# First GEMM of a two-layer trunk: order of its loads, source of x's split, and where its norm's squares are summed

## The reference

```
def rms_norm(x, g):
    y = x * lax.rsqrt(jnp.mean(x * x, axis=-1, keepdims=True) + EPS)
    return y * g

u = rms_norm(h, norm_mix_g[0])              # h = x, 512 x 1024
proj = u @ w_in                             # 1024 x (512 + 256 + 32)
c_q, c_kv, k_r = proj[..., :512], proj[..., 512:768], proj[..., 768:]
q  = rms_norm(c_q, g_q) @ w_uq
kv = rms_norm(c_kv, g_kv) @ w_ukv
k_r = apply_rope(k_r, cos, sin)             # cos, sin from positions
```

## Time and profile before

| | |
|---|---|
| median of the runs | 1299.8 us |
| profiled execution | 1299.99 us, its span 1298.2 us |
| busy share of the span | PE 95%, VectorE 52%, ScalarE 35%, GpSimd 22% |
| chain that ended last | PE 79%, VectorE 8%, issue 6%, ScalarE 3%, GpSimd 2% |
| granted TensorE clock, mean | 0.975 |
| PE busy in the first of 40 slices (32.5 us each), and in the second | 0.6, 0.8 |

### The profile page before, as it was taken

One profiled execution on the slowest core, in us unless ns is written; L12 is line 12 of the kernel. 1 busy time (PEld: TensorE's weight loads), 2 busy tenths in 40 slices (PEclk: granted clock), 3 DMA queues, 4 the chain that ended last, 5 costly groups with the idle time before them and its releaser, 6 DMA issues.

```text
span 1298.2 us, 15828 instructions
## 1 busy us (share of the span) xinstructions
PE 1231.2 (95%) x5829; PEld 1016.0 (78%) x5829; DVE 675.5 (52%) x958; ACT 455.1 (35%) x725; POOL 281.1 (22%) x252
## 2 busy tenths in 40 slices
PE   6889999899999999999999998889999999999997
PEld 5667777678888888888889986676888888888885
DVE  6867888744533434434457544974443343343432
ACT  4336666543212212222343235652322221221232
POOL 4222222222201102002112134552220020110211
PEclk8999999899999999999999998988999999999998
DMA  5201011222233332232233331011323223223221
GB/s 159 60 22 28 23 26 25 94 68 94 97 98 97 98 97 97 97 97 97 67 99 99 113 97 47 27 41 38 99 91 102 94 97 100 94 97 97 97 66 65
DMA packets 113888, 104.00 MB, mean 80 GB/s; under 512 B 20935, under 2 KB 112165, under 8 KB 113837
## 3 DMA queue, kind: packets, MB, share of 16 engines
q1 hardware_dynamic: 113344, 102.98, 25.1%
q10 hardware_dynamic: 492, 0.31, 0.1%
HBM read 101.17 MB, written 2.11 MB: 80 GB/s over the span
## 4 chain that ended last, share of the span: by engine, by line
PE 79%; DVE 8%; issue 6%; ACT 3%; POOL 2%; ACTq 0%; DMA 0%; DVEq 0%; POOLq 0%
PE ps L1466 24%; PE ps L1468 24%; PE ps L1467 24%; DVE nmax L1109 2%; POOL xl L568 1%; DVE xl L968 1%; DVE qtmp L1101 1%; ACT prob L712 1%; ACT uh L726 1%; DVE rinv L1114 1%; ACT whi L636 1%; DVE diag L1382 1%; ACT xh L698 0%; PE ps L1716 0%; PE ps L1717 0%
## 5 line engine op out<-in xcount | busy, mean ns | idle before, releaser
L963 DVE TENSOR_TENSOR wlo<-raw,whi 128x2048 fp32r<-128x2048 f32 (+2 forms) x89 | 194.4, 2188 | 157.3 <-ACT whi L636 157.3
L1466 PE MATMUL ps<-xl,whi 128*128 128x512 f32 (+1 forms) x688 | 270.7, 393 | 3.2 <-DVE krot L1048 3.2
L636 ACT CAST whi<-raw 128x2048 fp32r<-128x2048 f32 (+4 forms) x150 | 184.7, 1259 | 246.3 <-PE ps L1468 237.7
L1467 PE MATMUL ps<-xh,whi 128*128 128x512 f32 (+1 forms) x688 | 268.5, 390 | 0.0
L1468 PE MATMUL ps<-xh,wlo 128*128 128x512 f32 (+1 forms) x688 | 268.3, 390 | 0.0
L1466 PE MATMUL ps<-ul,whi 128*128 128x512 f32 x608 | 237.2, 390 | 1.2 <-POOL wlo L516 1.2
L1468 PE MATMUL ps<-uh,wlo 128*128 128x512 f32 x608 | 236.6, 389 | 0.0
L1467 PE MATMUL ps<-uh,whi 128*128 128x512 f32 x608 | 236.5, 389 | 0.0
L546 POOL TENSOR_TENSOR ul<-sq,uh 128x512 fp32r<-128x512 f32 x64 | 83.7, 1309 | 521.1 <-ACT uh L815 521.1
L1191 DVE TENSOR_TENSOR h<-ps,h 128x512 f32<-128x512 f32 x80 | 55.0, 690 | 199.3 <-PE ps L1468 192.6
L1466 PEld LDWEIGHTS ps<-xl,whi 128*128 128x128 f32 (+1 forms) x688 | 128.9, 187 | 32.0 <-issue 4.9
(11 more groups left out here) (234 smaller groups left out, 1648.0 us busy)
## 6 DMA issues: line engine op xcount, KB each, us to landing
raw<-in_mlp_w SPq DMA_DIRECT2D x64, 1024.0 KB, 5.1
raw<-in_mlstm_w_in SPq DMA_DIRECT2D x12, 1024.0 KB, 5.3
raw<-in_mla_w_o SPq DMA_DIRECT2D x4, 1024.0 KB, 5.0
raw<-in_mlstm_w_o SPq DMA_DIRECT2D x4, 1024.0 KB, 5.0
raw<-in_mla_w_in SPq DMA_DIRECT2D x3, 1024.0 KB, 5.4
raw<-in_mla_w_uq SPq DMA_DIRECT2D x16, 192.0 KB, 2.5
x_tok<-in_x SPq DMA_DIRECT2D x4, 512.0 KB, 5.6
mb<-m_rows SPq DMA_DIRECT2D x8, 256.0 KB, 3.4
```

Source lines behind the costliest of these rows:

```text
L636: last = sc.copy(hi, src)
L963: last = v.tensor_tensor(lo, src, hi.bitcast(F32), ALU.subtract)
L1466: mm(o, ah, bl, start=first, stop=False)
L1467: mm(o, ah, bh, start=False, stop=False)
```

## The change

Loads: N_KV's strip is issued first, ahead of x. Only the mixer gains are still loaded by ScalarE, with a semaphore of their own (`gain_in`); all other small loads move to SP, behind x and N_KR, and ahead of N_Q. PE transposes the mixer gains first, and all parameters again after the kr tile.

x's split: the transposed tile goes to banks 2 to 5 (`x_bank`). ScalarE makes `xh` and VectorE `xl` straight from PSUM; `h` is copied for tiles 0 to 5 by VectorE and for 6 and 7 by ScalarE. PE interleaves: after the `whi` products of tile k it transposes tile k + 4 (k < 4), or does the `wlo` products of two tiles (k >= 4).

Low parts of the weights: N_KV's moves from VectorE to GpSimd, N_Q + 1's from GpSimd to VectorE.

Norm: ScalarE squares `x_tok` (tokens on the partitions) in four activations of 128x1024 that also give the row sums; GpSimd's seven additions and PE's sum for this norm are gone. The spread stands before k = 5 of the kr product. The first half of the angle computation moves ahead of the norm's steps on VectorE.

```diff
--- before.py
+++ after.py
@@ -65,18 +65,19 @@
 T_O, T_WO2 = T_GATE + 17, T_GATE + 25
 T_MLP[1] = T_GATE + 33
 RING = 4
+H_ACT = 6
 B_Q, B_KV, B_S, B_PT, B_PV = 0, 1, 2, 4, 6
 B_ST, B_NUM, B_BCH, B_DEN, B_STAT = 4, (3, 7), 0, 2, 6
 B_OUT, B_BC, B_COL = 4, 6, 7
 
 
 NORM_MIX0, NORM_KV, NORM_CQ, NORM_MLP0, NORM_MIX1, NORM_MLP1, NORM_FIN = range(7)
-NORM_TILES = [KD, KVRANK // P, QRANK // P, KD, KD, KD, KD]
+NORM_TILES = [0, KVRANK // P, QRANK // P, KD, KD, KD, KD]
 
 
 def adds_before(norm):
 
-    return sum(n - 1 for n in NORM_TILES[:norm])
+    return sum(max(n - 1, 0) for n in NORM_TILES[:norm])
 
 
 def strip_over(n, gemm_done, q_mm):
@@ -134,6 +135,7 @@
         r_b = sb("r_b", [P, S])
         diag = sb("diag", [P, 2, S])
         var = sb("var", [P, 4])
+        x_sum = sb("x_sum", [P, 4])
         rcol = sb("rcol", [P, 4])
         rope_c = sb("rope_c", [P, 2])
         gate_b = sb("gate_b", [MH, 4])
@@ -254,9 +256,13 @@
         def bank(b):
             return ps[:, b, :]
 
+        def x_bank(m):
+
+            return bank(2 + m % RING)
+
 
         x_in = [sem(f"x_in{i}") for i in range(4)]
-        par_in = sem("par_in")
+        gain_in, par_in = sem("gain_in"), sem("par_in")
         pos_in = sem("pos_in")
         raw_full = [sem(f"raw_full{s}") for s in range(2)]
         whi_ready, wlo_ready = sem("whi_ready"), sem("wlo_ready")
@@ -393,13 +399,24 @@
                 return w[:, c:c + width].rearrange("(k p) n -> p k n", p=P)
 
             w_in = a["mla_w_in"][0]
+            load(N_KV, cols(w_in, QRANK))
             for i in range(4):
                 sp.dma_start(x_tok[:, :, 256 * i:256 * i + 256],
                              a["x"][0, :, 256 * i:256 * i + 256].rearrange("(t p) n -> p t n", p=P)) \
                     .then_inc(x_in[i], 16)
-            sp.wait_ge(par_in, 128)
-            load(N_KV, cols(w_in, QRANK))
             sp.dma_start(kr_raw(raw[1]), cols(w_in, QRANK + KVRANK, ROPE)).then_inc(raw_full[1], 16)
+            sp.dma_start(rope_c[:], a["rope_const"]).then_inc(pos_in, 16)
+            sp.dma_start(pos_i[:], a["positions"].broadcast_to([P, S])).then_inc(pos_in, 16)
+            sp.dma_start(gate_b[:, 0:1], a["mlstm_i_b"].rearrange("l h -> h l")).then_inc(pos_in, 16)
+            sp.dma_start(gate_b[:, 1:2], a["mlstm_f_b"].rearrange("l h -> h l")).then_inc(pos_in, 16)
+            for at, src in ((G_MLP, a["norm_mlp_g"].rearrange("l (m p) -> (l m) p", p=P)),
...
+                sp.dma_start(prow[at:at + src.shape[0], :], src).then_inc(par_in, 16)
             load(N_Q, cols(w_in, 0))
             load(N_Q + 1, cols(w_in, 256))
             slot_free(N_VA)
@@ -507,8 +524,6 @@
                 pool.wait_ge(var_ready, norm + 1)
                 g.tensor_tensor(rcol[:], var[:], mhalf[:, 0:4], ALU.pow).then_inc(rcol_ready, 1)
 
-            norm_adds(NORM_MIX0)
-            norm_pow(NORM_MIX0)
             def strip_low(n, kind, p=0):
 
                 pool.wait_ge(whi_ready, p * 2 + (n + 1))
@@ -516,9 +531,9 @@
                     last = g.tensor_tensor(lo, src, hi.bitcast(F32), ALU.subtract)
                 last.then_inc(wlo_ready, 1)
 
+            strip_low(N_KV, "full")
+            norm_pow(NORM_MIX0)
             norm_adds(NORM_KV)
-            pool.wait_ge(wlo_ready, N_Q + 1)
-            strip_low(N_Q + 1, "full")
             norm_pow(NORM_KV)
             norm_adds(NORM_CQ)
             norm_pow(NORM_CQ)
@@ -611,19 +626,8 @@
             own = Own(act, act_own)
             sc = nc.scalar
 
-            for at, src in ((G_MIX, a["norm_mix_g"].rearrange("l (m p) -> (l m) p", p=P)),
...
+            act.dma_start(prow[G_MIX:G_MLP, :], a["norm_mix_g"].rearrange("l (m p) -> (l m) p", p=P)) \
+                .then_inc(gain_in, 16)
 
             def split(n, kind="full", i=0, over=0, arrived=0):
 
@@ -656,12 +660,21 @@
                 sc.activation(xh[:, m, :], h[:, m, :], ACT.Copy, scale=pcol[:, gain + m:gain + m + 1]) \
                     .then_inc(xh_new, 1)
 
+            split(N_KV)
             act.wait_ge(par_ready, 1)
             for m in range(KD):
-                if m == 4:
-                    split(N_KV)
-                update(0, NORM_MIX0, G_MIX, m)
+                act.wait_ge(gemm_done, m + 1)
+                last = sc.activation(xh[:, m, :], x_bank(m), ACT.Copy, scale=pcol[:, G_MIX + m:G_MIX + m + 1])
+                if m >= H_ACT:
+                    last = sc.copy(h[:, m, :], x_bank(m))
+                last.then_inc(xh_new, 1)
             split(N_KR, "kr")
+            for t in range(TT):
+                last = sc.activation(sq[:, :, :].rearrange("p c s -> p (c s)"), x_tok[:, t, :], ACT.Square,
+                                     accum_out=x_sum[:, t:t + 1])
+                if t < TT - 1:
+                    own.link(last)
+            last.then_inc(stat_col, 1)
             split(N_Q)
             for m in range(2):
                 act.wait_ge(gemm_evac, T_IN + m + 1)
@@ -973,10 +986,15 @@
                 dve.wait_ge(xh_new, 8 * group + m + 1)
                 low(xl[:, m, :], h[:, m, :], xh[:, m, :], pcol[:, gain + m:gain + m + 1]).then_inc(x_ready, 1)
 
-            def stat_diag(norm, width):
+            def par_columns(n, c0, c1):
+                dve.wait_ge(par_t, n)
+                v.tensor_copy(pcol[:, c0:c1], ps[:, B_COL, c0:c1]).then_inc(par_ready, 1)
+                dve.wait_ge(par_ready, n)
+
+            def stat_diag(norm, width, sums=None):
 
                 dve.wait_ge(stat_col, norm + 1)
-                v.tensor_scalar(var[:], ps[:, B_COL, 0:4], 1.0 / width, EPS, ALU.mult, ALU.add) \
+                v.tensor_scalar(var[:], ps[:, B_COL, 0:4] if sums is None else sums, 1.0 / width, EPS, ALU.mult, ALU.add) \
                     .then_inc(var_ready, 1)
                 dve.wait_ge(rcol_ready, norm + 1)
                 for t in range(TT):
@@ -990,33 +1008,14 @@
                 dve.wait_ge(rbc_ready, norm + 1)
 
 
+            par_columns(1, G_MIX, G_MLP)
             for m in range(KD):
-                dve.wait_ge(gemm_done, m + 1)
-                v.tensor_copy(h[:, m, :], bank(m % RING)).then_inc(gemm_evac, 1)
-                if m == RING - 1:
-                    dve.wait_ge(par_t, 1)
-                    v.tensor_copy(pcol[:], ps[:, B_COL, 0:PCOLS]).then_inc(par_ready, 1)
-                    dve.wait_ge(par_ready, 1)
-                    for lead in range(m):
-                        x_low(0, G_MIX, lead)
-                elif m >= RING:
-                    x_low(0, G_MIX, m - 1)
-            x_low(0, G_MIX, KD - 1)
-            split(N_KV)
+                dve.wait_ge(xh_new, m + 1)
+                if m < H_ACT:
+                    v.tensor_copy(h[:, m, :], x_bank(m))
+                low(xl[:, m, :], x_bank(m), xh[:, m, :], pcol[:, G_MIX + m:G_MIX + m + 1]).then_inc(gemm_evac, 1)
+            dve.wait_ge(wlo_ready, N_KR)
             split(N_KR, "kr")
-
-            stat_diag(NORM_MIX0, D)
-            stat_row(NORM_MIX0, r_a)
-
-            def scaled(t, dst, r):
-
-                dve.wait_ge(gemm_done, t + 1)
-                return v.tensor_tensor(dst, bank(t % RING), r[:], ALU.mult)
-
-            for m in range(2):
-                scaled(T_IN + m, ckv[:, m, :], r_a).then_inc(gemm_evac, 1)
-            split(N_Q)
-
 
             dve.wait_ge(pos_in, 64)
             own.link(v.tensor_copy(ang[:], pos_i[:]))
@@ -1027,6 +1026,19 @@
                 own.link(v.scalar_tensor_tensor(out=ang[:], in0=turn[:], scalar=-part, in1=ang[:],
                                                 op0=ALU.mult, op1=ALU.add))
 
+            stat_diag(NORM_MIX0, D, x_sum[:])
+            split(N_Q)
+            stat_row(NORM_MIX0, r_a)
+
+            def scaled(t, dst, r):
+
+                dve.wait_ge(gemm_done, t + 1)
+                return v.tensor_tensor(dst, bank(t % RING), r[:], ALU.mult)
+
+            for m in range(2):
+                scaled(T_IN + m, ckv[:, m, :], r_a).then_inc(gemm_evac, 1)
+            par_columns(2, G_MLP, PCOLS)
+
             own.link(v.tensor_scalar(ang[:], ang[:], PI_IN, -PI_IN, ALU.min, ALU.max))
             own.link(v.tensor_scalar(turn[:], ang[:], np.pi / 2, -2 * np.pi, ALU.is_gt, ALU.mult))
             own.link(v.scalar_tensor_tensor(out=turn[:], in0=ang[:], scalar=np.pi / 2, in1=turn[:],
@@ -1034,6 +1046,7 @@
             own.link(v.tensor_scalar(turn[:], turn[:], PI_IN, -PI_IN, ALU.min, ALU.max))
             v.tensor_scalar(gate_b[:, 2:4], gate_b[:, 0:2], 1.0 / CAP, None, ALU.mult).then_inc(ang_ready, 1)
 
+            split(N_Q + 1)
             stat_diag(NORM_KV, KVRANK)
 
             v.memset(tab[0:64, :], SCALE)
@@ -1510,48 +1523,55 @@
 
 
             pe.wait_ge(consts, 1)
-            for m in range(KD):
-                if m == RING:
-                    pe.wait_ge(par_in, 128)
-                    tr(ps[:, B_COL, 0:PCOLS], prow[:, :], ident[0:PCOLS, 0:PCOLS]).then_inc(par_t, 1)
+            pe.wait_ge(gain_in, 16)
```

(74 more changed lines are left out.)

## The result

The changed kernel took 1280.34 us (median of four runs, 1279.87 to 1285.31) beside four runs of the kernel before with a median of 1299.47; the ratio is 0.9877, 95% interval 0.9847 to 0.9907. In six more runs it took 1280.55 us, against 1297.26 (17 runs), ratio 0.9883 (0.9851 to 0.9916).

A forecast was written before the change was run, and what follows sets the result against it. PE, busy 95% of the span, was taken as the bound, with gains only where it idles or runs slowly before 69 us. T_IN+7 ending at 55.5 instead of 68.59 gave 1299.9 - 13.1 = 1286.8 us, 8-in-10 range 1283.5 to 1292.

The forecast's parts named there:

- Rival 6: Start of the data: x's 2.9 us delay is passed on in full and the later gap moves; no change, 1300; 2%.
- the nearer row: x's split: xl straight from PSUM priced like a PSUM subtraction beside a busy GpSimd, 0.70 us each, instead of 1.5 us.
- rival 4: First GEMM: xl at 1.5 us paces PE, 1289.8 us; or gains or ScalarE's table load delay the first tile, 1288; 8%.
- the 0.4 us that the sum allowed: First GEMM: 0.4 us added to 12.65 us of products and transposes for the rest of the slow spell.
- rivals 2 and 5: Rival 2 has its own line; 5: clock stays low through the first GEMM and kr, 11.1 to 31 us, 1302.5 us; 3%.
- rival 2: First GEMM: a slow spell from 11.1 us, 4.4 us at half pace, 2.2 us lost less 0.4 counted, 1288.6 us; 17%.
- the rule cited in the prediction: Transposes do not count as clock-gate activity, so the slow spell would begin with the first product; the prediction held the trace against it.
- the 0.7 us ahead of the spread: kr product: PE reaches its wait at 27.5 us, diag comes at 28.2, so PE idles 0.7 us.
- the two values that the text gave: Start of T_IN+4: 31.6 us, or 30.8 if the cast of the positions is not stretched as beside GpSimd.
- Rival 3: Stall before T_IN+6 survives since VectorE has no slack; 3 us with a new slow spell of 1.7 give 1291.5; 12%.
- The step that failed: After 68.59 us: everything untouched, so the 13.1 us gained by T_IN+7's end carries over to the whole time within 0.2 us.
- Its own sign of failure: The forecast fails as a whole if x lands after 9 us, or if something after 69 us gives time back.

The follow-up runs named there:

- the last experiment: Changed kernel with x's four loads ahead of N_KV's weights again and N_KV cast between tiles 3 and 4 of x: 1288.4 us (one run).
- the two undone parts: Changed kernel with the first half of the angles back behind the second gain copy: 1290.2 us; separately, with N_Q + 1's low part back on GpSimd: 1281.1 us.
- n = 4: Both kernels with 4 spare products on PE ahead of tile T_IN+7: kernel before 1297.9 us, changed kernel 1283.0 us.
- n = 8: Both kernels with 8 spare products on PE ahead of tile T_IN+7: kernel before 1298.4 us, changed kernel 1282.7 us.
- the two with spare products in the heads: Both kernels with 6 spare products ahead of each diagonal-matrix wait in the mLSTM heads but the last: kernel before 1296.2 us, changed kernel 1282.9 us.
- the pair with all waits filled: Both kernels with spare products in the heads' waits, the last wait and the two before the first head: kernel before 1293.14 us, changed kernel 1279.34 us.

## Why the prediction was right in the mechanism and wrong in the number

**Start of the data.** Weights cast from 6.49, x at 8.02, gains at 4.27: 0.3 us later than worked out. Rival 6 falls: the delay of x is real, and the last experiment shows that x alone, earlier, gains nothing. SP's eleven small DMAs were issued by 13.1 us and not by 8.5 (the first took 2.87 us to issue); this cost nothing, as N_Q's cast at 24.96 us waited for PE.

**The first GEMM.** First product at 11.52 (11.1), kr at 24.71 (24.1). xl straight from PSUM took 0.74 us beside GpSimd, whose split took 4.56: the nearer row was the right one, and rival 4 falls. VectorE's first xl and copies, with the later work on it:

```profile
10.03 0.69 DVE L1015 COPY h<-ps 128x512 f32<-128x512 f32 x1 [5.29 <-ACT xh L667]
10.64 0.74 DVE L982 SCALAR_TENSOR_TENSOR xl<-ps,pcol,xh 128x512 fp32r<-128x512 f32 x1
...
21.28 0.42 DVE L1021 CAST ang<-pos_i 128x512 f32<-128x512 int32 x1
...
23.18 2.15 DVE L1026 SCALAR_TENSOR_TENSOR ang<-turn,ang 128x512 f32<-128x512 f32 x3
25.36 0.17 DVE L997 TENSOR_SCALAR var<-x_sum 128x4 f32<-128x4 f32 x1
26.67 0.88 DVE L1001 TENSOR_SCALAR diag<-ident,rcol 128x128 f32<-128x128 f32 x4 [1.14 <-POOL rcol L525]
```

**The clock rule.** The first product (11.52 to 12.09 us) still ran at half pace, and from 12.09 us the pace was the full one (rounds of 1.36 us: 12.87, 14.23; worked out was 1.34), after nothing but the gains' small transposition, 16 transposes of x and that product. In other executions of the same code the half pace lasted until up to 13.2 us. So the 0.4 us that the sum allowed was about right, and rivals 2 and 5 fall: the 4.4 us of half pace that rival 2 put behind 11.1 are not there. (Its reason, that every spell lasts about that, was wrong as well: those of the kernel before last 3.4 to 10.2 us.) This and the kernel before, where the second 16 transposes ran at twice the pace of the first 16 with no product ahead of them, speak against the rule cited in the prediction. The Trainium skill says that a transpose does not count as TensorE activity in the same way (TensorE: Matmul & The Clock Gate, Part 4: PE-mode transpose); for these float32 transposes the measurement decides against it.

**The norm.** The squares took 1.06 us and 0.19 more for reading each sum, 4.7 us in all, ending at 24.5, still hidden, by 0.9 us (2.2 forecast). The cast of the positions took 0.42 us (1.52 before, beside GpSimd) and the multiply-adds 2.15 (6.41). So diag was ready at 27.55 where 28.2 was forecast, and PE, which came there later than forecast, did not idle the 0.7 us ahead of the spread; T_IN+4 began at 31.22, between the two values that the text gave.

**Up to T_IN+7.** T_IN+6 at 44.27 (44.6), V products at 55.27 (55.5), PE idle 0.16 us before T_IN+6. That the mark was met within 0.2 us is in part luck: PE was 0.6 us late at kr, and the idle 0.7 us ahead of the spread did not come. Rival 3 did not come, but the two undone parts show how close it was: with 3.9 us of VectorE's work moved back PE idled 3.18 us on krot, and with one clamp slowed beside GpSimd 1.67 us.

**The step that failed** is the one that carried this over to the whole: "Everything after 68.59 us is untouched", and the sum "1299.9 - 13.1", with "a difference taken from the trace carries over within 0.2 us". The code behind is untouched, but its time is not: the clock there differs from execution to execution, and the prediction put this at nothing. Its own sign of failure, "if something after 69 us gives time back", came true in the profiled pair. Three parts of the 6.5 us between 1286.8 and 1280.3:
- The base: 1299.9 was one execution, and 1299.8 the median of three runs that happened to lie high; 53 runs have a mean of 1296.9. That is 3.0 us, and no property of the change.
- The worth: 13.8 (medians) to 14.1 us (means) with most of the chance taken out, against 13.1. Single traces give less: in the five pairs (as they are, n = 4, n = 8, and the two with spare products in the heads) the lead at the V products is 12.4 to 13.3 us, mean 12.8, and at the first head 11.6 to 13.8, mean 12.9. The profiled pair above has the largest of each. The forecast of 13.1 lies between the two, so this part of the sum was right within 1 us, and nothing shows that attention adds to it.
- The rest, some 2.5 us, is where the changed kernel's median lies: seven of ten runs are in its lower group, whose times lie 1.3 us under its own mean, and that mean is 1.1 us lower than 1296.9 less 14.1, which is within the uncertainty of the means (1.7). Whether the earlier start makes the lower group likelier is not settled: without spare products in the heads the means differ by 14.8 to 15.2 us, with them by 13.6 and 14.1, and about 1 us could be the change's own doing in the tail.

In the profiled pair the same is read from the trace: 13.8 us up to the first heads, 5.8 behind them, of which the pair with all waits filled leaves none (1278.0 and 1290.9 us of span, 12.9 apart).

## What to carry to other kernels

Where the end is set by an idle stretch and not by the amount of work, list what each engine has queued ahead of the awaited instruction, and move from there whatever has slack elsewhere; that sum held here to 0.2 us over 55 us, with two errors of 0.6 and 0.7 us against each other. A price measured beside a busy GpSimd is not the price without it (4.69 against 0.43 us for one clamp). And before a time is forecast to a few tenths of a per cent, know how far the kernel's own executions lie apart and whether they follow the granted clock: three runs that agree are not that knowledge.
